# Longer weight runs and 64-row tiles in a two-layer mixer and expert step

## What is computed

```python
q, k, v = ...                      # GDN: gated delta net, 4 heads of 128, chunks of 64, both directions
lower = jnp.where(strict, einsum('bhnid,bhnjd->bhnij', k_beta, k) * decay, 0.0)
a_intra = jnp.where(incl, einsum('bhnid,bhnjd->bhnij', q, k) * decay, 0.0)
...
# GLA: gated linear attention, 4 heads of 64 keys and 128 values, chunks of 64, both directions
o = einsum('bhcd,bhde->bhce', qd_c, S) + einsum('bhij,bhje->bhie', a_c, v_c)
S = S * gt_c[..., :, None] + einsum('bhcd,bhce->bhde', kt_c, v_c)
...
# differential attention: two score maps of 64 dims per head
s = einsum('bqhsd,bkhsd->bshqk', qb, kf) * DIFF_DH ** -0.5
w = softmax(s)[:, 0] - lam * softmax(s)[:, 1]
...
# merge, output projection, layer norm; then top-2 of 16 experts with d_ff 512
act = silu(einsum('nd,edf->nef', tok, w_gate)) * einsum('nd,edf->nef', tok, w_up)
out = einsum('nef,efd->nd', act * gates[..., None], w_down)
```

## Time and profile before

| | us |
|---|---|
| median of three runs | 2394.07 (2390.28 to 2397.73) |
| the profiled execution's own time | 2394.11 |
| its span, first to last instruction | 2392.1 |
| PE busy | 2168.5 (91%) |
| DVE, ACT, POOL busy | 807.4, 459.1, 215.7 |
| mean granted TensorE clock | 0.965 |

### The profile page before, as it was taken

How to read it: one execution, slowest core, us unless ns; L and a number is a source line. 1 busy time by engine, 2 the same in 40 slices (tenths; PEclk the granted TensorE clock), 3 DMA queues, 4 the chain that set the end, 5 groups by cost and what they waited for, 6 DMA issues and landing times.

```text
span 2392.1 us, 25335 instructions
## 1 busy us (share of the span) xinstructions
PE 2168.5 (91%) x9696; PEld 1197.1 (50%) x9696; DVE 807.4 (34%) x1602; ACT 459.1 (19%) x865; POOL 215.7 (9%) x222
## 2 busy tenths in 40 slices
PE   4999989999899979999799998999999979999994
PEld 1647875545444444344354787554544454344342
DVE  0535661614211421111553566161421251111115
ACT  0232123123200211011123212412320121011011
POOL 3023430000000000000002344000000000000000
PEclk8999999999999999999998999999999989999997
DMA  9421052142532259999722005213133229999993
GB/s 326 142 79 36 1 189 70 49 144 76 193 135 92 108 194 359 349 348 365 281 71 81 35 1 189 70 49 114 36 123 105 72 88 351 348 348 355 360 350 122
DMA packets 197474, 407.08 MB, mean 170 GB/s; under 512 B 6178, under 2 KB 6498, under 8 KB 197264
## 3 DMA queue, kind: packets, MB, share of 16 engines
q1 hardware_dynamic: 193136, 393.65, 46.5%
q0 software_dynamic: 4256, 12.28, 1.7%
HBM read 401.72 MB, written 4.19 MB: 170 GB/s over the span
## 4 chain that ended last, share of the span: by engine, by line
PE 77%; DMA 12%; DVE 5%; ACT 3%; issue 2%; SPq 1%; POOL 0%; DVEq 0%; POOLq 0%
PE bank L397 20%; DMA ring<-in_exp_w_up 10%; PE bank L556 8%; PE bank L902 6%; PE bank L930 6%; PE bank L407 5%; PE bank L890 5%; PE bank L509 5%; PE bank L818 5%; PE bank L940 2%; DMA ring<-in_w_mod 2%; PE bank L443 2%; PE bank L592 1%; PE bank L768 1%; PE bank L712 1%
## 5 line engine op out<-in xcount | busy, mean ns | idle before, releaser
L397 PE MATMUL bank<-ring,xt 128*128 128x512 f32 x1152 | 503.2, 598 | 10.3 <-DVE shared L1860 7.0
L397 PEld LDWEIGHTS bank<-ring,xt 128*128 128x128 f32 x1152 | 219.8, 192 | 288.2 <-issue 285.5
L902 PE MATMUL bank<-ring,shared 128*64 128x512 f32 x1280 | 290.5, 597 | 52.6 <-DMA ring<-in_exp_w_gate 31.5
L902 PEld LDWEIGHTS bank<-ring,shared 128*64 128x64 f32 x1280 | 86.9, 137 | 249.5 <-issue 163.7
L556 PE MATMUL bank<-shared 128*128 128x128 f32 x1408 | 175.1, 278 | 7.0 <-DVE shared L1705 4.8
L556 PEld LDWEIGHTS bank<-shared 128*128 128x128 f32 x1408 | 166.1, 192 | 15.1 <-issue 11.2
L1959 DVE TENSOR_TENSOR shared<-shared,bank 128x512 f32<-128x512 f32 x20 | 13.8, 688 | 437.8 <-PE bank L902 437.8
L930 PE MATMUL bank<-ring,shared 128*64 128x512 f32 x640 | 141.7, 595 | 1.2 <-issue 1.2
L890 PEld LDWEIGHTS bank<-qkvp,shared 128*128 128x128 f32 x1056 | 123.2, 197 | 20.2 <-issue 17.9
L407 PE MATMUL bank<-ring,xt 128*128 128x512 f32 x288 | 132.2, 606 | 0.0
L890 PE MATMUL bank<-qkvp,shared 128*128 128x128 f32 x1056 | 127.4, 282 | 3.8 <-DVE qkvp L1946 3.8
(11 more groups left out here) (348 smaller groups left out, 2190.2 us busy)
## 6 DMA issues: line engine op xcount, KB each, us to landing
ring<-in_exp_w_gate SPq DMA_DIRECT2D x80, 1024.0 KB, 8.0
ring<-in_exp_w_up SPq DMA_DIRECT2D x80, 1024.0 KB, 9.8
ring<-in_exp_w_down SPq DMA_DIRECT2D x80, 1024.0 KB, 10.7
ring<-in_w_in SPq DMA_DIRECT2D x32, 2048.0 KB, 9.9
ring<-in_w_mod SPq DMA_DIRECT2D x24, 2048.0 KB, 8.3
ring<-in_w_branch SPq DMA_DIRECT2D x6, 2048.0 KB, 7.9
ring<-in_w_out SPq DMA_DIRECT2D x4, 2048.0 KB, 7.8
shared<-in_ln_g POOLq DMA_DIRECT2D x4, 512.0 KB, 3.8
```

What stands on the lines that cost most here:

```text
L397: mm = pe.matmul(ps[:, 0:width], xtv[:, k, t * P:(t + 1) * P], w_of(k), start=(k == 0), stop=(k == KC - 1))
L902: mm = pe.matmul(ps[u * SLOTS:(u + 1) * SLOTS, :], xg[:, at:at + SLOTS], w[:, u, k, :], start=(part == k == 0), stop=(part == 1 and k == 3))
```

## The change

1. **Weights by longer runs.** Partition p of an expert's gate or up chunk now holds four neighbouring rows (8 KB in one run) and of a down chunk two neighbouring rows of 4 KB. `w_in` gets the same order of rows, still in pieces of 2 KB. Each dense load is two DMAs of 1 MB. So that rows match, `transpose_x`, eight of twelve `mod_columns` per layer and `turned` take every fourth column of their operand (a stride of 16 bytes) as the loaded operand.
2. **Down in two parts.** `output` walks the down weights by parts of rows and finishes both halves of its result at its end; SP's load of chunk 1 waits for a new semaphore at the same point of PE's work.
3. **Transposes of broadcast columns.** `gate_rows` uses 16 transposes in place of 16 matmuls. In GDN the ones products and POOL's two products go; PE transposes broadcast columns instead, and in the first pair the second direction uses the first one's qk and kk.
4. **GLA by 64-row tiles.** Scores, inter and ds become tiles of 64 rows, two or four of which touch different rows or columns of the array; q is one copy; inter is added in PSUM to the product with v; the state has half the columns (four DVE updates become two of 128 rows). Both directions of a step are issued together, and DVE adds the outputs at the pair's end.
5. **Attention by 64-row tiles.** The two score maps are products of 64 rows each, and ACT copies q once.

```diff
+        xq = x[:, :].rearrange("p (t a q b) -> p t a q b", t=T, a=2, q=P)
...
-                        mm = pe.transpose(ps[:, t * P:(t + 1) * P], xv[:, t, k * P:(k + 1) * P], c("ident"))
+                        mm = pe.transpose(ps[:, t * P:(t + 1) * P], xq[:, t, k // 4, :, k % 4], c("ident"))
...
+                    cols = mrow[:, b * P:(b + 1) * P] if j // 2 in (2, 5) else mrow[:, :].rearrange("p (q b) -> p q b", b=4)[:, :, b]
...
-                            mm = pe.matmul(ps[:, b * P:(b + 1) * P], modv[:, l, i, cond:cond + 1].broadcast_to([P, P]), c("ident"),
-                                           start=True, stop=True)
+                            mm = pe.transpose(ps[:, b * P:(b + 1) * P], modv[:, l, i, cond:cond + 1].broadcast_to([P, P]), c("ident"))
...
+                def row_of(ps, at, ready):
+                    for h in range(H):
+                        mm = pe.transpose(ps[:, h * P:(h + 1) * P], col(at + h, 1).broadcast_to([P, P]), c("ident"))
...
-                        pe.wait_ge(sem("gdn_rows"), n + 1)
-                        pe.matmul(ps[:, :], c("ones"), gd(d, "y"), start=True, stop=True).then_inc(ready, 1)
+                        row_of(ps, GC + at, ready)
...
+                        if p == 0 and d == 1:
+                            fills["qk", n], fills["kk", n] = fills["qk", n - 1], fills["kk", n - 1]
+                            continue
...
+                    for d in range(DIR):
+                        for hp in range(2):
+                            at = (d * 2 + hp) * P
+                            for hh, (ps, ready) in enumerate(scores):
+                                rows = slice(hh * 64, hh * 64 + 64)
+                                mm = pe.matmul(ps[:, at:at + P], gl_k[rows, at:at + P], gl_q[rows, at:at + P], start=True, stop=True)
...
+                                for hh, (ps, ready) in enumerate(outs):
+                                    rows = slice(hh * 64, hh * 64 + 64)
+                                    mm = pe.matmul(ps[tok, at:at + P], gl_dec[rows, at + ch[d] * HALF:at + (ch[d] + 1) * HALF],
+                                                   gla_state(p, d)[rows, hp * P:(hp + 1) * P],
+                                                   start=False, stop=(step == hp == d == 1), skip_group_check=True)
...
+                                    mm = pe.matmul(ps[rows, hp * P:(hp + 1) * P], gl("k_tail")[tok, at:at + 64],
+                                                   gvv[tok, t, h * P:(h + 1) * P], start=True, stop=True)
...
-                            pe.matmul(ps[:, 0:hi - lo], dq_z(s, h), dk_all[:, h, :][:, lo:hi],
+                            rows = slice(s * DH, (s + 1) * DH)
+                            pe.matmul(ps[:, 0:hi - lo], dq_t[rows, h * P:(h + 1) * P], dk_all[rows, h, lo:hi],
...
-                        mm = pe.transpose(ps[:, m * P:(m + 1) * P], hact[:, m * P:(m + 1) * P], c("ident"))
+                        mm = pe.transpose(ps[:, m * P:(m + 1) * P], hact.rearrange("p (q m) -> p q m", m=4)[:, :, m], c("ident"))
...
+            in_rows = lambda w: w.rearrange("(a p b) n -> p a b n", a=2, b=4)
...
-                        src = rows(a["exp_w_gate" if j < 2 else "exp_w_up"][l, e])[:, part * 4:(part + 1) * 4, :]
+                        src = in_rows(a["exp_w_gate" if j < 2 else "exp_w_up"][l, e])[:, part]
                     else:
-                        src = rows(a["exp_w_down"][l, e])[:, :, part * W5:(part + 1) * W5]
+                        src = a["exp_w_down"][l, e].rearrange("(p m) n -> p m n", m=4)[:, part * 2:(part + 1) * 2, :]
...
-                pool.memset(u_att[:, 0:2 * W5], 0.0).then_inc(sem("dq_zeroed"), 1)
```

More of the change, by code:

```diff
@@ L255, in arrived @@
             n = place[key]
[L256 to L257 removed]
+            eng.wait_ge(slot_in[n % RING], 32 * (n // RING + 1))
             return n % RING
@@ L688, in _ @@
-                    for d, t in enumerate(tiles):
-                        ps, ready = take(pe, ("gla_av", l, p, d))
-                        drained(pe, ("gla_a", l, p, d))
-                        for h in range(H):
-                            mm = pe.matmul(ps[:, h * P:(h + 1) * P], gla_at(d)[:, h * P:(h + 1) * P],
-                                           gvv[:, t, h * P:(h + 1) * P], start=True, stop=True)
-                        mm.then_inc(ready, 1)
-                    for step in range(2):
-                        for d, t in enumerate(tiles):
-                            ch = step if d == 0 else 1 - step
-                            tok = slice(ch * HALF, (ch + 1) * HALF)
-                            ps, ready = take(pe, ("gla_inter", l, p, d, step))
-                            if step == 0 and d == 0:
-                                drained(pe, ("q_dec", l, p))
+                    scores = [take(pe, ("gla_a", l, p, hh)) for hh in range(2)]
@@ new lines, in _ @@
+                    outs = [take(pe, ("gla_o", l, p, hh)) for hh in range(2)]
+                    for hh, (ps, _) in enumerate(outs):
+                        drained(pe, ("gla_a", l, p, hh))
+                        for d, t in enumerate(tiles):
+                            for hp in range(2):
+                                h, at = hp * 2 + hh, (d * 2 + hp) * P
+                                pe.matmul(ps[:, at:at + P], gla_at_of(d, h), gvv[:, t, h * P:(h + 1) * P],
+                                          start=(d == hp == 0), stop=False, skip_group_check=True)
@@ L702, in _ @@
+                    for step in range(2):
+                        ch = (step, 1 - step)
+                        if step == 0:
+                            drained(pe, ("q_dec", l, p))
+                            if p == 0:
+                                pe.wait_ge(sem("gla_zeroed"), l + 1)
+                            elif p == 1:
+                                pe.wait_ge(sem("gla_state_in"), 64 * (l + 1))
+                        for d in range(DIR):
                             if step == 1:
@@ L718, in _ @@
-                            if step == 0 and d == 0:
-                                pe.wait_ge(sem("gla_decayed"), (l * 3 + p) * 4 + 4)
-                            for hp in range(2):
-                                at = (d * 2 + hp) * P
-                                mm = pe.matmul(ps[:, hp * 256:(hp + 1) * 256], gl("k_tail")[tok, at:at + P],
-                                               gvv[tok, t, hp * 256:(hp + 1) * 256], start=True, stop=True)
-                            mm.then_inc(ready, 1)
+                                tok = slice(ch[d] * HALF, (ch[d] + 1) * HALF)
@@ new lines, in _ @@
+                        if p == 2 and step == 1:
+                            continue
+                        if step == 0:
+                            pe.wait_ge(sem("gla_decayed"), (l * 3 + p) * 4 + 4)
+                        sums = [take(pe, ("gla_ds", l, p, d, step)) for d in range(DIR)]
+                        for hp in range(2):
+                            for hh in range(2):
+                                h = hp * 2 + hh
+                                rows = slice(hh * 64, hh * 64 + 64)
+                                for d, t in enumerate(tiles):
+                                    ps, ready = sums[d]
+                                    at = (d * 2 + hp) * P + hh * 64
+                                    tok = slice(ch[d] * HALF, (ch[d] + 1) * HALF)
+                                    mm = pe.matmul(ps[rows, hp * P:(hp + 1) * P], gl("k_tail")[tok, at:at + 64],
+                                                   gvv[tok, t, h * P:(h + 1) * P], start=True, stop=True)
+                                    if hp == hh == 1:
+                                        mm.then_inc(ready, 1)
@@ L1007, in load @@
                 slot = place[key] % RING
-                sp.dma_start((ring_dn if name == "branch" else ring_in)[slot], source[name](l, j)).then_inc(slot_in[slot], 16)
+                to, of = (ring_dn if name == "branch" else ring_in)[slot], source[name](l, j)
+                n = to.shape[1] // 2
+                for part in range(2):
+                    cut = slice(part * n, (part + 1) * n)
+                    sp.dma_start(to[:, cut, :], of[:, cut, :] if name in ("mod", "out", "branch") else of[:, part, :, :])\
+                        .then_inc(slot_in[slot], 16)
             def load_pair(l, j, experts):
@@ L1748, in _ @@
                         ins.then_inc(sem("gla_decayed"), 1)
-                    for d, t in enumerate(tiles):
-                        ps, free = full(dve, ("gla_a", l, p, d))
-                        if p == 0 and d == 0:
+                    for hh in range(2):
+                        ps, free = full(dve, ("gla_a", l, p, hh))
+                        if p == hh == 0:
                             dve.wait_ge(sem("gla_zeroed"), l + 1)
-                        dve.copy_predicated(h4(gla_at(d)), fan(c(f"sum{d}").bitcast(U32), H), h4(ps[:, :])).then_inc(free, 1)
```

233 lines of the change are left out of this document (120 added, 113 removed).

## The result

The changed kernel takes 2327.11 us (median of four runs, 2313.53 to 2331.16), the kernel before 2393.16 in the same runs: a ratio of 0.9712, 95% interval 0.9669 to 0.9756. That is 66 us less, where 39 were forecast; the time lies 3 us under the range (2330 to 2392). The span of the profiled execution falls from 2392.1 to 2323.0 us.

A forecast was written before the change was run, and what follows sets the result against it. PE was taken to bound the kernel (77% of the chain), with waits for expert weights. Terms -20 -11.5 -11 -2.4 -2.6 +7 +1.2 = -39.3 from 2394.1 gave 2355 us (2340 to 2370 at 0.55); range 2330 to 2392.

The forecast's parts named there:

- Long runs: -20: Experts' loop: 8 KB runs load faster, 0.35 us off each gate wait, 0.70 off each up wait; -20 us, bounds 0 and -51.1.
- The ring: Experts' loop: down half done frees a slot, chunks 1, 2 and 3 load in turn, second up half; waits total 51.1 us.
- The rule that HBM holds a core at about 358 GB/s: Experts' loop: 353 GB/s would be the limit and long runs gain 0; kept as a rival, 2375 us, chance 0.12.
- GLA: -11.5: GLA's six pairs: scores, inter and ds on 64-row tiles overlap twofold; -11.5 us, +17 without overlap, -23 at fourfold.
- The new waits: GLA: PE waits 1.1 us for masking, 1.9 for both directions' states, 1.6 at the sum in pairs two and three.
- Strides: +7: PE's strided loads take twice the time; eight mod_columns instructions grow by 0.57 us in twelve calls; +7 us, ends 0 and +45.
- some two loads are under way at a time: PE's loads: a doubled load gives cadences of only 190 ns (small matmul) and 142 ns (transpose).
- GDN: -2.4: GDN's six pair starts: DVE sets the path, PE's saved work is hidden; -2.4 us, bounds 0 and twice that.
- The 0.4: GDN pair start: POOL's products hold up DVE, so removing them saves 0.4 us in each of six pairs.
- Attention: -11: Attention: score maps halved by overlap, six second copies of q gone, tile changes cost something; -11 us, bounds -17 and +3.
- Gate rows: -2.6: Gate rows: 32 instructions become 16, paced by ACT's copies; -1.3 us in each of two layers, bounds 0 and -3.7.
- +1.2: End of the down product: PE waits for one ACT copy behind the last pair, +0.6 us in each layer.

The follow-up runs named there:

- experiments 1 to 3: Changed kernel with expert weights in 2 KB pieces again: gate, up and down 2360.74 us; gate and up alone 2362.09; down alone, with its old code, 2325.98.
- Experiment 6: Changed kernel with all sixteen instructions of a GLA inter step on one 64 x 64 tile: 2355.89 us, one run; that time isn't used.
- experiments 7 and 11: Changed kernel with the strided loads of mod_columns, hidden rows and x made contiguous: 2316.78 us; with ACT's write of modulation rows strided instead of PE's load: 2317.68.

## Why the prediction fell short

It named the right sign and most of the mechanisms, and two terms were half of what they should have been; together they miss 27.6 of the 29.8 us by which the span's fall of 69.1 differs from the forecast.

- **Long runs: -20, measured -36.5 in the experts' stages.** The step that failed is "at 389 GB/s 5.39 us" and "at 416 GB/s, which gives 5.04 us. That saves 0.35 us on the gate wait". The ring was right, as experiments 1 to 3 show; but chunk 1 was priced at rates read in other stretches, and it had neither of them. From half of the down product (1065.30 before, 1004.94 after, half of 7.09 behind its start), which frees its slot, to the second gate part it was 8.87 us and is now 7.81: 1.06 less and not 0.35. The first three us and the next four of this stretch before (the last columns are DMA share and GB/s):

```profile
1065.30:1068.30 3.00, 3.00 (x18) 1.00 (x16) 0.86 (x4) 0.60 (x1) 0.00 (x0) 1.00 0.38 95
1068.30:1072.30 4.00, 3.97 (x20) 1.09 (x16) 0.00 (x0) 0.60 (x1) 0.00 (x0) 1.00 1.00 359
```

and after, with 140 us of the loop:

```profile
1004.94:1007.94 3.00, 3.00 (x18) 1.01 (x16) 0.79 (x4) 0.27 (x1) 0.00 (x0) 1.00 0.62 153
1007.94:1011.94 4.00, 3.97 (x20) 1.09 (x16) 0.00 (x0) 0.92 (x2) 0.00 (x0) 1.00 1.00 422
940.00:1080.00 140.00, 136.47 (x674) 60.85 (x670) 23.79 (x52) 17.05 (x30) 0.00 (x0) 1.00 0.91 376
```

  The start, 95 and now 153 GB/s, was left out of the sum; by these rows it is worth some 0.4 us (an estimate). Behind it chunk 1 came at 359 and now at 422 GB/s (367 and 426 in the median of the 18 turns), not at 389 and 416; that is the other 0.7. (The stretch at 416 was no pure case of long runs: a fifth of its bytes came in 2 KB pieces.) The up wait's 0.82 us went in full (0.70 forecast). Over all pairs the gate waits fell by 17.8 us and the up waits by 18.5, where 6.7 and 13.3 were forecast. The rule that HBM holds a core at about 358 GB/s (the Trainium skill, "DMA: Bandwidth & Descriptors", section "Where 436 GB/s comes from") is not what binds here: the loop now moves 376 on average.
- **GLA: -11.5, measured -22.6 in its stages, 19 to 22 when it is put back.** The step that failed is "I take twofold overlap for the 64-row tiles, as the new order puts one row half against the other, and keep none and fourfold as ends". For the scores, on two 64 x 128 tiles, it was nearly right (1.16 us, 1.01 forecast); inter and ds lie on four 64 x 64 tiles, whose column halves run beside each other as well. Experiment 6 shows fourfold, and the end that was kept, -23, is the measured one. The new waits came as forecast: 1.1 for the masks (0.87 measured), 1.9 for the states (1.51), 1.6 at the sum of the next pair (1.30).
- **Strides: +7, measured +10 and +9** (experiments 7 and 11). The load became 1.7 times as long, not twice, but the cadence went to 240 ns and not to 190: the rule "some two loads are under way at a time" did not hold for the strided ones. That `turned` hides it was right.
- **GDN: -2.4, measured -6 by the time, -8 by the stages, -10 by the starts of the pairs.** The step that failed is "the pair's start is DVE's ... and PE fills the time with a dense product". The filling product, held back by PE's wait for POOL (0.81 us) and by the ones products, outlasted DVE's chain by 0.29 us (303.99 against 303.70), so PE's saved work counted as well. The 0.4 itself was there: DVE's chain begins 0.5 us earlier.
- **Attention: -11, measured -8.** The maps' overlap is twofold less 0.19 us a step, and 0.25 to 0.35 us of it reach a step, less than the 0.47 that the terms give (0.73 less twice 0.13); right within its bounds.
- **Gate rows: -2.6, measured -3.3.** From the gate rows to the output projection it was 7.49 us, and is 5.82 in both layers:

```profile
756.47 1.91 PE L495 MATMUL bank<-cst,modt 128*128 128x128 f32 x16
...
762.29 4.13 PE L406 MATMUL bank<-ring,xt 128*128 128x512 f32 x9 [1.19 <-ACT xt L1494]
```

- The **+1.2** for the end of the down product was not there: PE waits 0.77 us for ACT behind the last pair, before and after.

The range failed because the upper ends of two gains, each kept as a bound (-51.1 and -23), were left out of its lower end together.

## What to carry to other kernels

Where a transfer stands in a ring with a product (slot freed, load, next product), price it from the release of the slot to the product's start, start-up included, and not by a rate read in another stretch; only the transfers in that ring were worth longer runs here, and work moved into the wait was over half free. Products on four 64 x 64 tiles overlapped nearly fourfold, those on two 64 x 128 tiles 1.6 to 1.7 times, so half-empty 128-row products are worth cutting up; let an engine with time to spare, and not PE's loads, carry a stride.

## What the runs showed of the hardware

- Four 64 x 64 tiles ran sixteen f32 instructions of 128 columns in 0.49 us, 31 ns each; on one tile one started every 0.11 us, and instructions for a free tile started ahead of earlier ones for a busy tile. The order over the tiles made no difference there, with four in a row on a tile; for two 64 x 128 tiles, with eight in a row, it did (1.16 us in turn, 1.68 tile by tile).
- A stride of 16 bytes took a load of PE from 190 to 329 ns and a small matmul's cadence from 119 to 240 ns, a transpose's from 150 to 160; ACT's write of 512 columns with a step of 512 bytes took 1046 in place of 597 ns.
- In the three us behind the release of its slot chunk 1 (2 MB) came at 98 GB/s in 2 KB pieces of scattered rows, at 80 in 2 KB pieces out of one run, and at 149 in 8 KB pieces; in the next four us at 367, 403 and 426 (medians of 18 turns).
